# Shifting the start addresses of rounded weights and activations in five feed-forward networks

## The chip, the cores and the metric

One core of one Trainium2 chip. The metric is the device time of the program in microseconds (us). Several runs were timed and their median is quoted; one more execution was recorded by the hardware profiler, and all rows below come from it.

## What is computed

Three transformer layers run one after another on 256 tokens of width 1024. The first mixes with RWKV7 and NSA attention, the second with gated linear attention and FoX, the third with a latent sparse attention. Between them stand five SwiGLU networks: one behind the first layer's mixer, and one on either side of the second's and of the third's. Only these networks and the products around the mixers matter here:

```python
def swiglu(x, w_gate, w_up, w_down):
    return (jax.nn.silu(x @ w_gate) * (x @ w_up)) @ w_down

def swiglu_2(h, w_in, w_out):
    a, b = jnp.split(h @ w_in, 2, axis=-1)
    return (jax.nn.silu(a) * b) @ w_out

for layer in range(DEPTH_2):
    g = norm_g[layer]
    x = x + 0.5 * swiglu_2(rmsnorm(x, g[0]), ffn_w_in[layer, 0], ffn_w_out[layer, 0])
    ...
    x = x + 0.5 * swiglu_2(rmsnorm(x, g[2]), ffn_w_in[layer, 1], ffn_w_out[layer, 1])
```

Everything is float32, with an inner width of 2816.

## The kernel before

Each float32 operand of a large product is split into a rounded high part and a rest, both kept in the rounded 4-byte format `fp32r`, and a product is made of three passes (`PASSES`): high weights with high activations, rest of the weights with high activations, high weights with the rest of the activations. So every 128-by-128 tile of weights costs three matmuls.

A network (`ffn(f, norm)`, f from 0 to 4) is cut into `FC` = 22 chunks of 128 inner columns. For a chunk, the weights arrive by DMA in one slot of `ring` (3,072 floats per partition: 2,048 for gate and up, 1,024 for down). ScalarE rounds them into `w_gu[:, j, 0]` and `w_dn[:, j, 0]` (`hi_a` and `hi_b`, L1368 and L1374), VectorE writes the rests into `w_gu[:, j, 1]` and `w_dn[:, j, 1]` (`lo_a` and `lo_b`, L2028 and L2034); j is the chunk's parity. TensorE then runs `gate_up`: 2 results (gate, up) x 8 blocks k of the inner dimension x 3 passes = 48 matmuls, with a tile of `w_gu` standing in the array and 256 columns of `uT_r` moving through it. `uT_r[0]` is the high part `uT_h` of the normed and transposed activations, `uT_r[1]` the rest `uT_l`. VectorE and ScalarE turn the two results into `h` and its rest (`h_r`), and TensorE runs `down`: 4 parts x 3 passes = 12 matmuls with a tile of `h_r` standing and 512 columns of `w_dn` moving. A chunk is therefore 48 x 256 + 12 x 512 = 18,432 moving columns. In the loop TensorE runs `gate_up` of chunk c, then `down` of chunk c - 1. All matmuls go through one helper, so they carry its line, L498, in the profile; they are told apart by the names of their operands, the moving one first ("uT_h,w_gu": moving `uT_h`, standing `w_gu`).

The mixers' projections use the same three passes. Input projections take the high weights from `in_h`, `even_h` or `odd_h`, and the rest of the weights from `ring_r` (the ring itself, written back in place). Output projections keep a tile of `uT_h` or `uT_l` standing and move 512 columns of `out_h` or `ring_r`. Some small products take `gate_w` (24 columns standing), `odd_small` (8 columns) and, for one sum of FoX, a single column of `fox_head` repeated 128 times.

Addresses. `sb(name, shape)` allocates tensors one after another in each partition, every one at the next multiple of 32 bytes, and `over(name, shape, under, skip)` lays a second, rounded tensor over one of them, `skip` floats past its start. With the sizes of this kernel the tensors start at these bytes (in brackets: bytes past a multiple of 128): `uT` 32,896 (0), `yT` 41,088 (0), `inh` 49,280 (0), `gate_r` 61,568 (0), `ring` 63,104 (0), `ffb` 112,256 (0), `cst` 116,352 (0, with 4,662 floats), `wk` 138,336 (96). `uT_h` lies on `uT`, `uT_l` on `yT`, `in_h` on `inh`, `h_r` on `ffb`; `w_gu`, `w_dn`, `even_h`, `odd_h`, `out_h`, `fox_sum` and `fox_head` lie on `wk` at offsets that are multiples of 128 bytes. The strides from one tile to the next inside these tensors are multiples of 128 bytes, except in `gate_w` (96 bytes) and `odd_small` (32 bytes). So in every network before the change all rounded weights start 96 bytes past a multiple of 128 and all activations on one.

Of the kernel before, what the change touches and what calls it, by code (L numbers as in the profile page):

```python
# [7 lines left out]
F32 = mybir.dt.float32  # L8
F32R = mybir.dt.float32r
U8 = mybir.dt.uint8  # L10
ALU = mybir.AluOpType
# [84 lines left out]
def build(nc, x_in, wstream, gains, consts_in, masks_in, scratch, tri, inv, out):  # L96
    ctx = ExitStack()
    with ctx:
        at = {}

        def sb(name, shape, dt=F32):
            at[name] = nc.sbuf_base
            return ctx.enter_context(nc.sbuf_tensor(name, shape, dt))
# [17 lines left out]

        x = sb("x", [P, TT, D])
        xn = sb("xn", [P, TT, D])
        uT = sb("uT", [P, KC, T])
        yT = sb("yT", [P, KC, T])
        inh = sb("inh", [P, KC * 3 * P])
        gb = inh[:, 0:2 * D].rearrange("p (a b) -> p a b", b=D)
        sb("gate_r", [P, 2 * KC * 24])
        ring = sb("ring", [P, RING, SLOT])
        ffb = sb("ffb", [P, 4, T])  # L130
        cst = sb("cst", [P, NCONST])
        msk = sb("msk", [P, MASKS], U8)
        small = sb("small", [P, 256])
# [16 lines left out]

        ident = C("ident")

        w_gu = over("w_gu", [P, 2, 2, 2 * D], "wk")
        w_dn = over("w_dn", [P, 2, 2, D], "wk", 8 * D)
        h_r = over("h_r", [P, 2, 2, T], "ffb")
        ring_r = over("ring_r", [P, RING, SLOT], "ring")

        w_h = {"even": [over(f"even_h{i}", [P, KC, 3 * P], "wk", o) for i, o in enumerate((17408, 9728))],
# [329 lines left out]
        def slot(i):  # L488
            return ring[:, i % RING, :]
# [3 lines left out]
        def _(pe):  # L493
# [54 lines left out]

            PASSES = [(0, 0), (1, 0), (0, 1)]

            def gate_up(j, between=None):
                for m in range(2):
                    if m and between:
                        between()
                    for k in range(KC):
                        for n, (a, b) in enumerate(PASSES):
                            w = w_gu[:, j % 2, a, (m * KC + k) * P:(m * KC + k + 1) * P]
                            last = mm(ps[4 + 2 * m + j % 2][:, 0:T], w, uT_r[b][:, k, :],
                                      k == 0 and n == 0, k == KC - 1 and n == 2)
                    last.then_inc(s[("gu_gate", "gu_ps")[m]], 1)  # L560

            def first_gate_up(norm):

                for k in range(KC):
                    pe.wait_ge(s["uT_hi"], 16 * TN[norm] + 8 + k + 1)
                    for m in range(2):
                        for a in range(2):
                            mm(ps[4 + 2 * m][:, 0:T], w_gu[:, 0, a, (m * KC + k) * P:(m * KC + k + 1) * P],
                               uT_r[0][:, k, :], k == 0 and a == 0, False)
                for m in range(2):  # L570
                    for k in range(KC):
                        if not m:
                            pe.wait_ge(s["uT_lo"], 16 * TN[norm] + 8 + k + 1)
                        last = mm(ps[4 + 2 * m][:, 0:T], w_gu[:, 0, 0, (m * KC + k) * P:(m * KC + k + 1) * P],
                                  uT_r[1][:, k, :], False, k == KC - 1)
                    last.then_inc(s[("gu_gate", "gu_ps")[m]], 1)

            def spread_rstd(norm):
# [5 lines left out]
                if norm == 1:  # L584
                    mm(ps[1][0:16, 0:384], C("t5")[0:32, :], C("t5_onehot")[0:32, :]).then_inc(s["t5_ps"], 1)

            def down_part(j, t, half, start, stop):
                for n, (a, b) in enumerate(PASSES):
                    last = mm(ps[2 * t + half][:, :], h_r[:, j % 2, a, t * P:(t + 1) * P],
                              w_dn[:, j % 2, b, half * 512:(half + 1) * 512], start and n == 0, stop and n == 2)  # L590
                return last

            def down(j, start):
                for t, half in PARTS:
                    last = down_part(j, t, half, start, False)
                last.then_inc(s["down_done"], 1)

            def ffn(f, norm):
                q = FC * f

                def step(c, r=0):

                    pe.wait_ge(s["lo_a"], r + (q + c + 1))
                    if q + c >= 2:
                        pe.wait_ge(s["h_ready"], r + (q + c - 1))
                    if c == 0:
                        first_gate_up(norm)
                    else:
                        gate_up(c, (lambda: spread_rstd(norm)) if c == 1 else None)
                    if 0 < c < FC - 1:  # L610
                        pe.wait_ge(s["lo_b"], r + (q + c))
                        pe.wait_ge(s["h_ready"], r + (q + c))
                        if norm == 1 and c == 1:
                            pe.wait_ge(s["t5_sb"], 1)
                        down(c - 1, c == 1)
                step(0)
                step(1)
                with pe.Fori(0, 4 * LOOPS, 4) as r:
                    for j in range(4):
                        step(2 + j, r)  # L620
                for c in range(2 + 4 * LOOPS, FC):
                    step(c)

                n = NORM_AFTER_FFN[f]
                pe.wait_ge(s["lo_b"], q + FC - 1)
                pe.wait_ge(s["h_ready"], q + FC - 1)
                for t, half in PARTS[0:3]:
                    down_part(FC - 2, t, half, False, False)
                pe.wait_ge(s["lo_b"], q + FC)
                pe.wait_ge(s["h_ready"], q + FC)  # L630
                for t, half in PARTS[0:3]:
                    down_part(FC - 1, t, half, False, True).then_inc(s["acc_done"], 1)
                first_T(n, 0)
                down_part(FC - 2, 1, 1, False, False).then_inc(s["down_done"], 1)
                down_part(FC - 1, 1, 1, False, True).then_inc(s["down_done"], 1)
                first_T(n, 1)

            def piece(o, j):
# [647 lines left out]
        def _(act):  # L1286
# [676 lines left out]
        def _(v):  # L1963
# [60 lines left out]
            def lo_a(f, c, r=0):  # L2024

                q, i = FC * f, BASE[f"ffn{f}"] + c
                v.wait_ge(s["hi_a"], r + (q + c + 1))
                v.tensor_tensor(w_gu[:, c % 2, 1, :], slot(i)[:, 0:2 * D], w_gu[:, c % 2, 0, :].bitcast(F32),  # L2028
                                ALU.subtract).then_inc(s["lo_a"], 1)

            def lo_b(f, c, r=0):
                q, i = FC * f, BASE[f"ffn{f}"] + c
                v.wait_ge(s["hi_b"], r + (q + c + 1))
                v.tensor_tensor(w_dn[:, c % 2, 1, :], slot(i)[:, 2 * D:3 * D], w_dn[:, c % 2, 0, :].bitcast(F32),  # L2034
                                ALU.subtract).then_inc(s["lo_b"], 1)
                v.wait_ge(s["lo_b"], r + (q + c + 1))
                v.sem_inc(s[f"free{i % RING}"], 1)
# [14 lines left out]
            def ffn(f, scale):  # L2052
                q = FC * f

                def step(c, r=0):
                    n = q + c
                    h, hr = sg[:, c % 2, :], h_r[:, c % 2, :, :]
# [742 lines left out]
```

## Time and profile before

| | |
|---|---|
| median of 3 runs | 1424.02 us (1423.72 to 1424.87) |
| span of the profiled execution | 1422.4 us |
| TensorE matmuls busy | 1395.2 us, 98% |
| TensorE weight loads busy | 1286.2 us, 90% |
| VectorE busy | 944.7 us, 66% |
| ScalarE busy | 691.0 us, 49% |
| mean DMA rate | 168 GB/s |

The span runs from the first to the last instruction of the trace and is 1.6 us under the median of the timed runs. Matmuls overlap one another in the pipeline: one lasts 279 ns with 256 columns, but the next one starts before it ends. So their cost is read from the distance between two starts, not from their duration.

### The profile page before, as it was taken

What the parts mean: (1) busy time and instruction counts of PE and PEld (TensorE: products, weight loads), DVE (VectorE), ACT (ScalarE), POOL (GpSimd) and SP (SyncE); (2) the same over time, 40 slices, a digit from 0 to 9 for tenths busy, and PEclk for the clock granted to TensorE, in tenths of its full rate; (3) what the DMA queues carried; (4) which work ended last, traced back from release to release, by engine and by line L of the source; (5) the groups of instructions that cost most, each with busy time, mean ns of one, the idle gap of its engine ahead of it and who ended that gap; (6) DMA issues with size and microseconds to landing.
All of it is one profiled execution on the core that took longest, in us unless ns stands there. A gap on an engine that the chain in (4) does not pass through costs nothing. (4 is left out here: it accounts for less than half of the span.)

```text
span 1422.4 us, 25483 instructions
## 1 busy us (share of the span) xinstructions
PE 1395.2 (98%) x10044; PEld 1286.2 (90%) x10044; DVE 944.7 (66%) x1539; ACT 691.0 (49%) x1107; POOL 82.9 (6%) x137
## 2 busy tenths in 40 slices
PE   8999999999999999999999999999999999999997
PEld 8898888999989999899989999999998988899997
DVE  5778567766668666567577666676665676676665
ACT  6764545433454443376654433444433655643342
POOL 1030010000020000000000000100000123000000
PEclk9999999999999999999999999999999999999999
DMA  9344005645526555433356545365554423465540
GB/s 359 135 160 185 2 25 228 222 177 183 197 108 228 209 184 177 178 104 133 120 207 224 189 177 182 129 229 198 194 177 178 149 90 134 177 222 180 194 158 30
DMA packets 33069, 239.47 MB, mean 168 GB/s; under 512 B 6864, under 2 KB 13280, under 8 KB 14304
## 3 DMA queue, kind: packets, MB, share of 16 engines
q1 hardware_dynamic: 30320, 234.84, 45.6%
q10 hardware_dynamic: 2672, 3.58, 0.7%
q8 instruction: 51, 0.84, 0.2%
q14 instruction: 26, 0.21, 0.0%
HBM read 236.15 MB, written 2.25 MB: 168 GB/s over the span
## 5 line engine op out<-in xcount | busy, mean ns | idle before, releaser
L498 PE MATMUL ps<-uT_h,w_gu 128*128 128x256 f32 x3520 | 614.1, 279 | 2.5 <-ACT uT_h L1316 2.5
L498 PEld LDWEIGHTS ps<-uT_h,w_gu 128*128 128x128 f32 x3520 | 538.0, 188 | 13.8 <-issue 5.0
L498 PE MATMUL ps<-uT_l,w_gu 128*128 128x256 f32 x1760 | 478.8, 279 | 0.0
L498 PE MATMUL ps<-w_dn,h_r 128*128 128x512 f32 x1320 | 325.7, 396 | 0.3 <-DVE h_r L2070 0.3
L498 PEld LDWEIGHTS ps<-uT_l,w_gu 128*128 128x128 f32 x1760 | 325.5, 188 | 0.0
L498 PEld LDWEIGHTS ps<-w_dn,h_r 128*128 128x128 f32 x1320 | 239.6, 188 | 51.3 <-issue 1.4
L1368 ACT CAST w_gu<-ring 128x2048 fp32r<-128x2048 f32 x110 | 210.0, 1909 | 156.2 <-PE ps L498 155.6
L2028 DVE TENSOR_TENSOR w_gu<-ring,w_gu 128x2048 fp32r<-128x2048 f32 x110 | 252.1, 2292 | 35.2 <-ACT w_gu L1368 35.2
L2061 DVE TENSOR_TENSOR us<-ps,bc 128x256 f32<-128x256 f32 x110 | 46.5, 423 | 203.2 <-PE ps L498 203.2
L1381 ACT ACTIVATE wk<-wk 128x256 f32<-128x256 f32 x110 | 46.1, 419 | 260.7 <-DVE wk L2059 260.7
L1374 ACT CAST w_dn<-ring 128x1024 fp32r<-128x1024 f32 x110 | 115.7, 1052 | 82.8 <-PE ps L498 82.7
L2034 DVE TENSOR_TENSOR w_dn<-ring,w_dn 128x1024 fp32r<-128x1024 f32 x110 | 134.1, 1219 | 5.3 <-ACT w_dn L1374 5.1
L498 PE MATMUL ps<-uT_h,ring_r 128*128 128x256 f32 x408 | 114.4, 281 | 0.0
L498 PE MATMUL ps<-wk 128*128 128x64 f32 (+6 forms) x504 | 76.9, 303 | 1.9 <-DVE small L2337 0.7
L498 PEld LDWEIGHTS ps<-uT_h,ring_r 128*128 128x128 f32 x408 | 77.5, 190 | 0.6 <-issue 0.2
L2059 DVE TENSOR_TENSOR wk<-ps,bc 128x256 f32<-128x256 f32 x110 | 46.7, 425 | 35.8 <-PE ps L498 22.0
L498 PEld LDWEIGHTS ps<-wk 128*128 128x128 f32 (+3 forms) x504 | 56.1, 186 | 7.4 <-issue 2.0
L498 PE MATMUL ps<-ring_r,uT_h 128*128 128x512 f32 (+2 forms) x176 | 62.0, 353 | 0.0
L2064 DVE TENSOR_TENSOR wk<-wk,us 128x256 f32<-128x256 f32 x110 | 46.7, 425 | 7.7 <-ACT wk L1381 4.3
L498 PE MATMUL ps<-uT_h,in_h 128*128 128x256 f32 x176 | 50.5, 289 | 1.0 <-DVE ring_r L2021 1.0
L2070 DVE TENSOR_TENSOR h_r<-wk,h_r 128x256 fp32r<-128x256 f32 x110 | 46.8, 425 | 3.7
L498 PE MATMUL ps<-uT_l,in_h 128*128 128x256 f32 x176 | 48.7, 283 | 0.0
(398 smaller groups left out, 1696.0 us busy)
## 6 DMA issues: line engine op xcount, KB each, us to landing
ring<-wstream SPq DMA_DIRECT2D x144, 1536.0 KB, 6.6
cst<-consts_in SPq DMA_DIRECT2D x1, 2185.0 KB, 13.7
wk<-t_row ACTq DMA_DIRECT2D x1, 2048.0 KB, 8.0
wk<-masks_in SPq DMA_DIRECT2D x1, 1216.0 KB, 24.1
x<-x_in SPq DMA_DIRECT2D x2, 512.0 KB, 4.7
ring<-wstream SPq DMA_DIRECT2D x1, 1024.0 KB, 8.8
inh<-gains ACTq DMA_DIRECT2D x2, 512.0 KB, 9.6
tri_blocks<-wk SPq DMA_DIRECT2D x3, 256.0 KB, 2.8
```

Of the source, the lines that this page charges most:

```text
L498: return pe.matmul(o, l, r, start=start, stop=stop, skip_group_check=True)
L1368: act.copy(w_gu[:, c % 2, 0, :], slot(i)[:, 0:2 * D]).then_inc(s["hi_a"], 1)
L1374: act.copy(w_dn[:, c % 2, 0, :], slot(i)[:, 2 * D:3 * D]).then_inc(s["hi_b"], 1)
L1381: act.activation(sg[:, c % 2, :], sg[:, c % 2, :], ACT.Silu).then_inc(s["silu_ready"], 1)
L2028: v.tensor_tensor(w_gu[:, c % 2, 1, :], slot(i)[:, 0:2 * D], w_gu[:, c % 2, 0, :].bitcast(F32), ALU.subtract).then_inc(s["lo_a"], 1)
L2034: v.tensor_tensor(w_dn[:, c % 2, 1, :], slot(i)[:, 2 * D:3 * D], w_dn[:, c % 2, 0, :].bitcast(F32), ALU.subtract).then_inc(s["lo_b"], 1)
L2059: v.tensor_tensor(h, ps[4 + c % 2][:, 0:T], bc[:], ALU.mult).then_inc(s["gs_ready"], 1)
L2061: v.tensor_tensor(us[:], ps[6 + c % 2][:, 0:T], bc[:], ALU.mult).then_inc(s["us_ready"], 1)
L2064: v.tensor_tensor(h, h, us[:], ALU.mult).then_inc(s["h_mul"], 1)
L2070: v.tensor_tensor(hr[:, 1, :], h, hr[:, 0, :].bitcast(F32), ALU.subtract).then_inc(s["h_ready"], 1)
```

## The change

Three tensors (`uT`, `yT`, `ffb`) are allocated 16 floats longer. Each network gets its own views of the weights and activations: `W_SHIFT` moves `w_gu` and `w_dn` of network f by 8, 0, 24, 0 and 16 floats (32, 0, 96, 0 and 64 bytes), `U_SHIFT` moves `uT_h`, `uT_l` and `h_r` by 0, 8, 0, 16 and 0 floats (0, 32, 0, 64 and 0 bytes). The scratch `sg` lies 32 floats later. The instructions, their order, their sizes and their semaphores stay the same; only operand addresses differ.

```diff
@@ -121,13 +121,13 @@
 
         x = sb("x", [P, TT, D])
         xn = sb("xn", [P, TT, D])
-        uT = sb("uT", [P, KC, T])
-        yT = sb("yT", [P, KC, T])
+        uT = sb("uT", [P, KC * T + 16])[:, 0:KC * T].rearrange("p (k n) -> p k n", k=KC)
+        yT = sb("yT", [P, KC * T + 16])[:, 0:KC * T].rearrange("p (k n) -> p k n", k=KC)
         inh = sb("inh", [P, KC * 3 * P])
         gb = inh[:, 0:2 * D].rearrange("p (a b) -> p a b", b=D)
         sb("gate_r", [P, 2 * KC * 24])
         ring = sb("ring", [P, RING, SLOT])
-        ffb = sb("ffb", [P, 4, T])
+        ffb = sb("ffb", [P, 4 * T + 16])[:, 0:4 * T].rearrange("p (k n) -> p k n", k=4)
         cst = sb("cst", [P, NCONST])
         msk = sb("msk", [P, MASKS], U8)
@@ -150,9 +150,10 @@
 
         ident = C("ident")
 
-        w_gu = over("w_gu", [P, 2, 2, 2 * D], "wk")
-        w_dn = over("w_dn", [P, 2, 2, D], "wk", 8 * D)
-        h_r = over("h_r", [P, 2, 2, T], "ffb")
+        W_SHIFT, U_SHIFT, FFN_OF = (8, 0, 24, 0, 16), (0, 8, 0, 16, 0), {1: 0, 3: 1, 5: 2, 6: 3, 8: 4}
+        w_gu = [over(f"w_gu{f}", [P, 2, 2, 2 * D], "wk", n) for f, n in enumerate(W_SHIFT)]
+        w_dn = [over(f"w_dn{f}", [P, 2, 2, D], "wk", 8 * D + n) for f, n in enumerate(W_SHIFT)]
+        h_r = [over(f"h_r{f}", [P, 2, 2, T], "ffb", n) for f, n in enumerate(U_SHIFT)]
         ring_r = over("ring_r", [P, RING, SLOT], "ring")
 
@@ -163,7 +164,9 @@
         w_small = [over(f"even_small{i}", [P, KC * 40], "wk", 14336 + KC * 40 * i) for i in range(2)]
         wo_h = [over(f"out_h{i}", [P, SLOT], "wk", o) for i, o in enumerate((13312, 17408, 10240))]
         uT_r = [over("uT_h", [P, KC, T], "uT"), over("uT_l", [P, KC, T], "yT")]
-        sg = wk[:, 12 * D:12 * D + 2 * T].rearrange("p (a b) -> p a b", a=2)
+        uT_f = [[over(f"uT_h{f}", [P, KC, T], "uT", n), over(f"uT_l{f}", [P, KC, T], "yT", n)] if n else uT_r
+                for f, n in enumerate(U_SHIFT)]
+        sg = wk[:, 12 * D + 32:12 * D + 32 + 2 * T].rearrange("p (a b) -> p a b", a=2)
         ss = [small[:, 0:1], small[:, 1:2], small[:, 8:9]]
         ss3 = [small[:, 242:243], small[:, 243:244]]
@@ -548,31 +551,32 @@
 
             PASSES = [(0, 0), (1, 0), (0, 1)]
 
-            def gate_up(j, between=None):
+            def gate_up(f, j, between=None):
                 for m in range(2):
                     if m and between:
                         between()
                     for k in range(KC):
                         for n, (a, b) in enumerate(PASSES):
-                            w = w_gu[:, j % 2, a, (m * KC + k) * P:(m * KC + k + 1) * P]
-                            last = mm(ps[4 + 2 * m + j % 2][:, 0:T], w, uT_r[b][:, k, :],
+                            w = w_gu[f][:, j % 2, a, (m * KC + k) * P:(m * KC + k + 1) * P]
+                            last = mm(ps[4 + 2 * m + j % 2][:, 0:T], w, uT_f[f][b][:, k, :],
                                       k == 0 and n == 0, k == KC - 1 and n == 2)
...
@@ -584,15 +588,15 @@
                 if norm == 1:
                     mm(ps[1][0:16, 0:384], C("t5")[0:32, :], C("t5_onehot")[0:32, :]).then_inc(s["t5_ps"], 1)
 
-            def down_part(j, t, half, start, stop):
+            def down_part(f, j, t, half, start, stop):
                 for n, (a, b) in enumerate(PASSES):
-                    last = mm(ps[2 * t + half][:, :], h_r[:, j % 2, a, t * P:(t + 1) * P],
...
@@ -1313,7 +1317,7 @@
                 for c in range(KC):
                     if c % 4 == 0 or t and c % 2 == 0:
                         act.wait_ge(s["xT_ps"], 6 * TN[n] + (2 + c // 2 if t else c // 4) + 1)
-                    act.mul(uT_r[0][:, c, t * P:(t + 1) * P], xT_at(n, t, c), gain_c(n, c)).then_inc(s["uT_hi"], 1)
+                    act.mul(uT_f[FFN_OF.get(n, 0)][0][:, c, t * P:(t + 1) * P], xT_at(n, t, c), gain_c(n, c)).then_inc(s["uT_hi"], 1)
 
             def norm(n):
@@ -1365,13 +1369,13 @@
                 act.wait_ge(s[f"land{i % RING}"], rr + 16 * (i // RING + 1))
                 if q + c >= 2:
                     act.wait_ge(s["gu_ps"], r + (q + c - 1))
-                act.copy(w_gu[:, c % 2, 0, :], slot(i)[:, 0:2 * D]).then_inc(s["hi_a"], 1)
+                act.copy(w_gu[f][:, c % 2, 0, :], slot(i)[:, 0:2 * D]).then_inc(s["hi_a"], 1)
 
             def hi_b(f, c, r=0):
                 q, i = FC * f, BASE[f"ffn{f}"] + c
                 if q + c >= 2:
                     act.wait_ge(s["down_done"], r + (q + c - 1))
-                act.copy(w_dn[:, c % 2, 0, :], slot(i)[:, 2 * D:3 * D]).then_inc(s["hi_b"], 1)
+                act.copy(w_dn[f][:, c % 2, 0, :], slot(i)[:, 2 * D:3 * D]).then_inc(s["hi_b"], 1)
 
             def ffn(f, norm):
...
@@ -1982,8 +1986,9 @@
                         step = 2 if t else 4
                         v.wait_ge(s["uT_hi"], 16 * TN[n] + KC * t + c // step * step + step)
                         tk = slice(t * P, (t + 1) * P)
-                        v.scalar_tensor_tensor(uT_r[1][:, c, tk], xT_at(n, t, c), gain_c(n, c),
-                                               uT_r[0][:, c, tk].bitcast(F32), ALU.mult, ALU.subtract
+                        u = uT_f[FFN_OF.get(n, 0)]
+                        v.scalar_tensor_tensor(u[1][:, c, tk], xT_at(n, t, c), gain_c(n, c),
+                                               u[0][:, c, tk].bitcast(F32), ALU.mult, ALU.subtract
                                                ).then_inc(s["uT_lo"], 1)
 
...
```

The parts left out pass `f` to `gate_up`, `first_gate_up`, `down_part` and `down` and use `w_gu[f]`, `w_dn[f]`, `h_r[f]` and `uT_f[f]` in the same way.

## Rows read from the trace of the kernel before

**Rows 1.** The page, busy time by engine (share of the span, instructions) and clock by slice.

```profile
span 1422.4 us, 25483 instructions
...
PE 1395.2 (98%) x10044; PEld 1286.2 (90%) x10044; DVE 944.7 (66%) x1539; ACT 691.0 (49%) x1107; POOL 82.9 (6%) x137
...
PEclk9999999999999999999999999999999999999999
```

**Rows 2.** Waits of TensorE: engine, line, who released it, us in total, times, longest.

```profile
PE ps L498 <- DMA cst<-consts_in: 5.1, 1, 5.1
PE ps L498 <- DVE xn L1976: 3.3, 3, 1.2
PE ps L498 <- ACT uT_h L1316: 2.5, 5, 0.5
```

**Rows 3.** The five networks' stretches: busy us (instructions) by engine, clock, DMA share, GB/s.

```profile
core 0: us, PE busy (x) PEld busy (x) DVE busy (x) ACT busy (x) POOL busy (x), PEclk, DMA share, GB/s
226.00:413.50 187.50, 187.50 (x1337) 174.57 (x1338) 123.10 (x172) 81.10 (x86) 4.23 (x7) 1.00 0.56 203
...
1229.20:1415.00 185.80, 185.80 (x1324) 173.17 (x1324) 120.79 (x170) 76.81 (x81) 1.49 (x4) 1.00 0.45 165
```

**Rows 4.** Timeline of TensorE, one chunk of network 0: start, length, operation, operands, count.

```profile
258.35 0.40 PE L498 MATMUL ps<-uT_h,w_gu 128*128 128x256 f32 x2
...
263.95 2.96 PE L498 MATMUL ps<-w_dn,h_r 128*128 128x512 f32 x12
266.75 0.40 PE L498 MATMUL ps<-uT_h,w_gu 128*128 128x256 f32 x2
```

**Rows 5.** Timeline of TensorE in the first input projection.

```profile
24.94 0.28 PE L498 MATMUL ps<-uT_h,in_h 128*128 128x256 f32 x1
25.06 0.28 PE L498 MATMUL ps<-uT_h,ring_r 128*128 128x256 f32 x1
25.18 0.28 PE L498 MATMUL ps<-uT_l,in_h 128*128 128x256 f32 x1
...
26.02 0.28 PE L498 MATMUL ps<-uT_h,in_h 128*128 128x256 f32 x1
```

**Rows 6.** Timeline of TensorE in the second and third input projections, far rows.

```profile
613.15 0.28 PE L498 MATMUL ps<-uT_h,even_h 128*128 128x256 f32 x1
...
618.81 0.28 PE L498 MATMUL ps<-uT_h,even_h 128*128 128x256 f32 x1
...
1120.93 0.28 PE L498 MATMUL ps<-uT_h,odd_h 128*128 128x256 f32 x1
...
1126.19 0.28 PE L498 MATMUL ps<-uT_h,odd_h 128*128 128x256 f32 x1
```

**Rows 7.** Timeline of TensorE, products with 24 and 8 standing columns.

```profile
91.98 0.39 PE L498 MATMUL ps<-uT_h,gate_w 128*24 128x256 f32 x2
...
93.00 0.39 PE L498 MATMUL ps<-uT_h,gate_w 128*24 128x256 f32 x2
...
1110.28 0.39 PE L498 MATMUL ps<-uT_h,odd_small 128*8 128x256 f32 x2
...
1110.98 0.39 PE L498 MATMUL ps<-uT_h,odd_small 128*8 128x256 f32 x2
```

**Rows 8.** Timeline of TensorE, the sum with one repeated column standing.

```profile
636.92 1.90 PE L498 MATMUL ps<-fox_sum,fox_head 128*128 128x256 f32 x15
```

**Rows 9.** Groups by line: rounding on ScalarE and VectorE, us busy, mean ns, idle before.

```profile
L1368 ACT CAST w_gu<-ring 128x2048 fp32r<-128x2048 f32 x110 | 210.0, 1909 | 156.2 <-PE ps L498 155.6
L2028 DVE TENSOR_TENSOR w_gu<-ring,w_gu 128x2048 fp32r<-128x2048 f32 x110 | 252.1, 2292 | 35.2 <-ACT w_gu L1368 35.2
```

**Rows 10.** One tile's matmuls: count, ns min/median/max, first and last start.

```profile
L498 PE MATMUL ps<-uT_h,in_h x176: 277/283/468, 15.1 to 91.3; 128*128 128x256 f32 x176
```

More of the change, by code:

```diff
@@ L562, in first_gate_up @@
             def first_gate_up(norm):
+                f = FFN_OF[norm]
                 for k in range(KC):
@@ L567, in first_gate_up @@
                         for a in range(2):
-                            mm(ps[4 + 2 * m][:, 0:T], w_gu[:, 0, a, (m * KC + k) * P:(m * KC + k + 1) * P],
-                               uT_r[0][:, k, :], k == 0 and a == 0, False)
+                            mm(ps[4 + 2 * m][:, 0:T], w_gu[f][:, 0, a, (m * KC + k) * P:(m * KC + k + 1) * P],
+                               uT_f[f][0][:, k, :], k == 0 and a == 0, False)
                 for m in range(2):
@@ L573, in first_gate_up @@
                             pe.wait_ge(s["uT_lo"], 16 * TN[norm] + 8 + k + 1)
-                        last = mm(ps[4 + 2 * m][:, 0:T], w_gu[:, 0, 0, (m * KC + k) * P:(m * KC + k + 1) * P],
-                                  uT_r[1][:, k, :], False, k == KC - 1)
+                        last = mm(ps[4 + 2 * m][:, 0:T], w_gu[f][:, 0, 0, (m * KC + k) * P:(m * KC + k + 1) * P],
+                                  uT_f[f][1][:, k, :], False, k == KC - 1)
                     last.then_inc(s[("gu_gate", "gu_ps")[m]], 1)
@@ L585, in spread_rstd, with down @@
                     mm(ps[1][0:16, 0:384], C("t5")[0:32, :], C("t5_onehot")[0:32, :]).then_inc(s["t5_ps"], 1)
-            def down_part(j, t, half, start, stop):
+            def down_part(f, j, t, half, start, stop):
                 for n, (a, b) in enumerate(PASSES):
-                    last = mm(ps[2 * t + half][:, :], h_r[:, j % 2, a, t * P:(t + 1) * P],
-                              w_dn[:, j % 2, b, half * 512:(half + 1) * 512], start and n == 0, stop and n == 2)
+                    last = mm(ps[2 * t + half][:, :], h_r[f][:, j % 2, a, t * P:(t + 1) * P],
+                              w_dn[f][:, j % 2, b, half * 512:(half + 1) * 512], start and n == 0, stop and n == 2)
                 return last
-            def down(j, start):
+            def down(f, j, start):
                 for t, half in PARTS:
-                    last = down_part(j, t, half, start, False)
+                    last = down_part(f, j, t, half, start, False)
                 last.then_inc(s["down_done"], 1)
@@ L608, in step @@
                     else:
-                        gate_up(c, (lambda: spread_rstd(norm)) if c == 1 else None)
+                        gate_up(f, c, (lambda: spread_rstd(norm)) if c == 1 else None)
                     if 0 < c < FC - 1:
@@ L614, in step @@
                             pe.wait_ge(s["t5_sb"], 1)
-                        down(c - 1, c == 1)
+                        down(f, c - 1, c == 1)
                 step(0)
@@ L627, in ffn @@
                 for t, half in PARTS[0:3]:
-                    down_part(FC - 2, t, half, False, False)
+                    down_part(f, FC - 2, t, half, False, False)
                 pe.wait_ge(s["lo_b"], q + FC)
@@ L631, in ffn @@
                 for t, half in PARTS[0:3]:
-                    down_part(FC - 1, t, half, False, True).then_inc(s["acc_done"], 1)
+                    down_part(f, FC - 1, t, half, False, True).then_inc(s["acc_done"], 1)
                 first_T(n, 0)
-                down_part(FC - 2, 1, 1, False, False).then_inc(s["down_done"], 1)
-                down_part(FC - 1, 1, 1, False, True).then_inc(s["down_done"], 1)
+                down_part(f, FC - 2, 1, 1, False, False).then_inc(s["down_done"], 1)
+                down_part(f, FC - 1, 1, 1, False, True).then_inc(s["down_done"], 1)
                 first_T(n, 1)
@@ L2027, in lo_a @@
                 v.wait_ge(s["hi_a"], r + (q + c + 1))
-                v.tensor_tensor(w_gu[:, c % 2, 1, :], slot(i)[:, 0:2 * D], w_gu[:, c % 2, 0, :].bitcast(F32),
+                v.tensor_tensor(w_gu[f][:, c % 2, 1, :], slot(i)[:, 0:2 * D], w_gu[f][:, c % 2, 0, :].bitcast(F32),
                                 ALU.subtract).then_inc(s["lo_a"], 1)
@@ L2033, in lo_b @@
                 v.wait_ge(s["hi_b"], r + (q + c + 1))
-                v.tensor_tensor(w_dn[:, c % 2, 1, :], slot(i)[:, 2 * D:3 * D], w_dn[:, c % 2, 0, :].bitcast(F32),
+                v.tensor_tensor(w_dn[f][:, c % 2, 1, :], slot(i)[:, 2 * D:3 * D], w_dn[f][:, c % 2, 0, :].bitcast(F32),
                                 ALU.subtract).then_inc(s["lo_b"], 1)
@@ L2056, in step @@
                     n = q + c
-                    h, hr = sg[:, c % 2, :], h_r[:, c % 2, :, :]
+                    h, hr = sg[:, c % 2, :], h_r[f][:, c % 2, :, :]
                     v.wait_ge(s["gu_gate"], r + (n + 1))
```

## The prediction

> **What bounds the kernel.** I read the shares of busy time first, then TensorE's waits, then the stretches of the five networks, and last the distances between matmul starts. TensorE is busy for 1395.2 of 1422.4 us and its clock stands at the full level, 2.4 GHz, in all 40 slices [rows 1]. What it waits for is small and outside the networks' loops: the longest wait is 5.1 us for the constants, the next groups add up to 3.3 and 2.5 us [rows 2]. The first network takes 187.5 us with TensorE busy for 187.50, the last 185.8 with 185.80, and the three between them, whose rows are not shown, lie at 186.4 to 188.5 [rows 3]. VectorE needs 123 us of such a stretch and ScalarE 81 [rows 3]. So inside the networks nothing but the pace of the matmul stream sets the time, and every nanosecond on a matmul arrives at the end.
>
> That pace is what the change can touch. One chunk runs from 258.35 to 266.75 us, 8.40 us [rows 4]. It holds 48 matmuls of 256 columns and 12 of 512, that is 72 units of 256 columns, so 116.7 ns per unit. Its gate and up part alone, 258.35 to 263.95, is 5.60 / 48 = 116.7, and its down part, 263.95 to 266.75, is 2.80 / 24 = 116.7: the same price in both parts. 256 columns at 2.4 GHz are 106.7 ns. So about 10 ns per unit, 9%, is lost somewhere in the stream although nobody waits. A network has 22 x 72 = 1,584 units and all five have 7,920, so 1 ns per unit is 1.6 us in one network and 7.9 us in all.
>
> **Does the loss depend on addresses?** The kernel before has other combinations of the start addresses, and they are not equally fast:
> - The first input projection has weights (`in_h`, `ring_r`) and activations all on multiples of 128 bytes. From 24.94 to 26.02 us there are 9 matmuls, 120.0 ns each, and every distance shown is 0.12 us [rows 5].
> - The networks have weights 96 bytes past and activations on a multiple: 116.7 ns [rows 4].
> - The second and third input projections take two of three weight tiles at 96 bytes past (`even_h`, `odd_h`) and one on a multiple (`ring_r`). 48 matmuls from 613.15 to 618.81 us give 117.9 ns, 45 from 1120.93 to 1126.19 give 116.9 [rows 6].
> - Strides off the multiple: with 24 standing columns 9 matmuls from 91.98 to 93.00 us take 113.3 ns each, with 8 columns 6 from 1110.28 to 1110.98 take 116.7 [rows 7].
> - One repeated column standing, both operands 96 bytes past: 15 matmuls in 1.90 us, of which the last is 0.28 long, so 1.62 / 14 = 115.7 ns [rows 8].
>
> The same shape costs between 113.3 and 120.0 ns at one clock. The order among the full 128-column cases, all equal 120.0, one in three equal 117.9 or 116.9, none equal 116.7, is what one would see if the standing and the moving operand got in each other's way when their addresses agree. I take that as the mechanism. It isn't shown, since these stages also differ in strides.
>
> **Where the change puts things.** The three longer tensors hold 64 bytes more each. So `yT` starts 64 bytes later, everything from `inh` to `ffb` 128 bytes later, and `cst` and what follows, `wk` included, 192 bytes later. `wk` moves from 96 to 32 bytes past a multiple of 128, and the shifts come on top. By network, as weights; `uT_h`, `uT_l`; `h_r`: network 0 has 64; 0, 64; 0. Network 1 has 32; 32, 96; 32. Network 2 has 0; 0, 64; 0. Network 3 has 32; 64, 0; 64. Network 4 has 96; 0, 64; 0. These are not the addresses that the change is described with (0, 96, 64, 96, 32): that list leaves the 192 bytes out.
>
> **The sum.** Two ways to count what "agree" means:
> - Modulo 64. Then networks 0 and 2 have everything on multiples of 64, as the first input projection has, and go from 116.7 to 120.0 ns: 1,584 x 3.3 = 5.2 us each, 10.4 us. Networks 3 and 4 keep weights at an odd and activations at an even multiple of 32, as now: 0. Network 1 has all at odd multiples of 32, which no full-width row shows; its bounds are 113.3 and 120.0 ns, so -5.4 to +5.2 us, and the nearest row, both operands at 96 [rows 8], gives 115.7, or -1.6 us. That row has hardly any weights to read, so I take 0. The first input projection stays on multiples of 64: 0.
> - Modulo 128. Networks 1 and 2 have weights and `uT_h` alike in two passes of three and weights and `h_r` alike in all. With 3.3 ns for all three passes, 2.2 for two and 1.1 for one, the gate and up part costs 1,056 x 2.2 = 2.3 us and the down part 528 x 3.3 = 1.7 us, 4.1 us (from unrounded terms) per network and 8.1 for two. In network 0 only `uT_l` is like the weights: 1,056 x 1.1 = 1.2 us. Networks 3 and 4 have no like pair: 0. In the first input projection `uT_l` leaves the multiple: it has 176 matmuls of each pass with `in_h` [rows 10], and with 16 output-side ones per pass some 576 in all, at -1.1 ns, -0.6 us. Together +8.7 us.
>
> Both come to about the same, and I take 9.5 us. The profiled span would go from 1422.4 to 1431.9 us and the median, 1.6 us above it, from 1424.0 to 1433.5 us. Network 1 alone moves this by 5 us, and if only network 2 pays it is 4: 1428 to 1439 for this case.
>
> **Edits costed at nothing.** No instruction, wait or transfer is added. ScalarE's rounding of a chunk's gate and up weights takes 1,909 ns and VectorE's rest 2,292 ns [rows 9], in a chunk of 8.40 us; ScalarE and VectorE have 106 and 64 us of slack per network [rows 3]. If a shifted output made each of these a tenth slower, 0.2 us per chunk, that slack would cover it. The cover is gone only if the matmuls got faster by a third. The output projections and the second and third input projections read `wk` at 32 instead of 96 bytes past: for both ways of counting that is no new agreement with the activations on a multiple, 0; a change of 1 ns on their some 1,500 units would be 1.5 us. The later place of `sg`, a whole 128 bytes, changes nothing in any of this.
>
> The Trainium skill speaks against the whole mechanism. Its page SBUF — State Buffer says under Specifications (TRN2) that SBUF is read in 16-byte lines, and under Who interferes with whom that TensorE has separate read ports for the moving and the standing operand and never waits on anyone. All shifts are multiples of 32 bytes, so by it a start would stay on a line and the result would be no change, 1424.0 us. This trace does not settle it, but 120.0 against 116.7 ns [rows 4, 5] is a difference that this rule leaves unexplained. The page TensorE: Matmul & The Clock Gate gives under Back-to-back issue gap N/2.4 + 2.5 ns, 109.2 ns for 256 columns; an estimate by it would put the most that five networks could gain at 7,920 x 7.5 ns, about 59 us. No row reaches that.
>
> **The rivals.**
> - Nothing depends on these addresses, and the 120.0 ns come from something else in that stage, such as its 1,536-byte stride between tiles. For it: the five networks lie within 1.5% of each other, and the down part, whose operands have other roles and strides, pays the same 116.7. Against it: the second input projection has the same 1,536-byte stride and 117.9. Time: 1424.0 us.
> - Faster. Some distance between the streams that the kernel never had at full width (64 bytes, or 32 on the other side) is cheaper than today's. The place is the three networks with such a distance, 0, 3 and 4, and with network 1 four of five are new in some pair. The price goes down to the 113.3 ns of [rows 7]: 1,584 x 3.4 = 5.4 us per network. Two such networks and no dear one give 1424.0 - 10.8 = 1413.2 us; all five give 1397. It decides as soon as the networks that win outnumber those that lose. For it: 113.3 was reached with mixed residues. Against it: only with 24 columns to load, and 8 columns gave 116.7.
> - The change isn't what it is called, since the pads move `wk`. If the addresses were those of its name, networks 0 and 2 would still be the ones with all on multiples of 64, and modulo 64 the sum is the same 10.4 us. So this rival has no time of its own.
>
> **How the numbers follow.** Agreement costs, slower: 0.50, at 1433.5 us. No dependence, or gains and losses that cancel: 0.20, at 1424.0. Faster: 0.30, at 1413. What a measurement of this kernel can tell from no change is about 0.2%, 2.8 us. The range of 8 in 10 runs from 1411 us, where the two-network gain is held and only larger ones are out, to 1440 us, where network 1 pays in full.
>
> **What would show it.** In the profile after, the length of one chunk in each network: 8.40 us today, 8.64 us (72 x 120.0 ns) in networks 0 and 2 if modulo 64 is right, about 8.6 in 1 and 2 if modulo 128 is right, 8.40 in 3 and 4. If all five stay at 8.40 us, addresses don't matter. If any shows less than 8.35, there is a cheaper distance and the forecast's sign is in doubt. The clock has to stay at its full level, and waits of TensorE in the networks have to stay near zero; otherwise the cause is another.

## The result

The changed kernel takes 1428.12 us (median), the kernel before 1424.85 us in the same session; the ratio is 1.0023 with a 95% interval of 1.0014 to 1.0033. It is slower by 3.3 us. The forecast was slower by 9.5 us: the side is right, the size is almost three times too large, and, as the experiments show, most of the reasons behind it are wrong. All times compared below are of undisturbed executions; one of the ten of the first scan took 4854 us, where the others took 1427 to 1429, and is left out of its interval.

The page of the profile after, busy time and clock, is close to [rows 1], with 4.5 us more of TensorE:

```profile
span 1426.7 us, 25483 instructions
...
PE 1399.7 (98%) x10044; PEld 1293.5 (91%) x10044; DVE 945.4 (66%) x1539; ACT 689.6 (48%) x1107; POOL 82.7 (6%) x137
...
PEclk9999999999999999999999999999999999999999
```

The waits of TensorE (engine and line, who released it, us in total, times, longest) are those of [rows 2] to 0.1 us, so no large wait was added:

```profile
PE ps L501 <- DMA cst<-consts_in: 5.1, 1, 5.1
PE ps L501 <- DVE xn L1980: 3.2, 3, 1.2
PE ps L501 <- ACT uT_h L1320: 2.5, 5, 0.5
```

The time is in the pace of the matmuls. This is the timeline of TensorE in the changed kernel, one chunk of each network, read as [rows 4]: the first line of three is the start of gate and up, the second the start of down, the third the start of the next chunk.

```profile
318.21 0.40 PE L501 MATMUL ps<-uT_h,w_gu 128*128 128x256 f32 x2
...
323.86 2.93 PE L501 MATMUL ps<-w_dn,h_r 128*128 128x512 f32 x12
326.63 0.40 PE L501 MATMUL ps<-uT_h,w_gu 128*128 128x256 f32 x2
...
507.98 0.40 PE L501 MATMUL ps<-uT_h,w_gu 128*128 128x256 f32 x2
...
513.63 2.88 PE L501 MATMUL ps<-w_dn,h_r 128*128 128x512 f32 x12
516.35 0.40 PE L501 MATMUL ps<-uT_h,w_gu 128*128 128x256 f32 x2
...
818.36 0.40 PE L501 MATMUL ps<-uT_h,w_gu 128*128 128x256 f32 x2
...
824.00 2.94 PE L501 MATMUL ps<-w_dn,h_r 128*128 128x512 f32 x12
826.78 0.40 PE L501 MATMUL ps<-uT_h,w_gu 128*128 128x256 f32 x2
...
1007.75 0.40 PE L501 MATMUL ps<-uT_h,w_gu 128*128 128x256 f32 x2
...
1013.45 2.96 PE L501 MATMUL ps<-w_dn,h_r 128*128 128x512 f32 x12
1016.25 0.40 PE L501 MATMUL ps<-uT_h,w_gu 128*128 128x256 f32 x2
...
1323.47 0.40 PE L501 MATMUL ps<-uT_h,w_gu 128*128 128x256 f32 x2
...
1329.13 2.96 PE L501 MATMUL ps<-w_dn,h_r 128*128 128x512 f32 x12
1331.93 0.40 PE L501 MATMUL ps<-uT_h,w_gu 128*128 128x256 f32 x2
```

The chunks last 8.42, 8.37, 8.42, 8.50 and 8.46 us; every one was 8.40 before, as in [rows 4]; the rows of the other four aren't shown. Network 1 is faster, the others are slower. The table has the median over some 20 chunks of each network, per 256 columns, worked out from the starts in the trace like this: gate and up is first start to second start over 48, down is second to third over 24. In network 3 two kinds of chunk alternate (118.7 and 118.4 ns in gate and up, 116.5 and 116.2 in down), and the row has their middle. Distances are weights minus the other operand, modulo 256 bytes; why 256 comes with the experiments.

| network | weights - `uT_h`, `uT_l` | gate and up, ns | weights - `h_r` | down, ns | chunk, us | against before |
|---|---|---|---|---|---|---|
| before, all five | 224, 224 | 116.7 | 224 | 116.7 | 8.400 | |
| 0 | 192, 128 | 117.7 | 64 | 115.4 | 8.420 | +0.020 |
| 1 | 128, 64 | 117.8 | 0 | 113.3 | 8.373 | -0.027 |
| 2 | 0, 192 | 117.7 | 128 | 115.8 | 8.427 | +0.027 |
| 3 | 96, 32 | 118.5 | 224 | 116.4 | 8.484 | +0.084 |
| 4 | 224, 160 | 118.0 | 96 | 116.5 | 8.460 | +0.060 |

The last column sums to 0.164 us, times 22 chunks 3.6 us, near the 3.3 us of the medians. Gate and up lost in every network, between 1.0 and 1.9 ns, and down won in all five, from 0.1 to 3.4 ns. The first input projection [rows 5], at 120.0 ns before in its earlier and later parts alike, now has two paces. From 24.87 to 33.59 us 72 matmuls take 121.1 ns each, and from 66.95 to 68.01 us 9 take 117.8:

```profile
24.87 0.28 PE L501 MATMUL ps<-uT_h,in_h 128*128 128x256 f32 x1
...
33.59 0.28 PE L501 MATMUL ps<-uT_h,in_h 128*128 128x256 f32 x1
...
66.95 0.28 PE L501 MATMUL ps<-uT_h,in_h 128*128 128x256 f32 x1
...
68.01 0.28 PE L501 MATMUL ps<-uT_h,in_h 128*128 128x256 f32 x1
```

Over the whole stage the two nearly cancel: about -0.3 us, an estimate from the lengths of the stretches.

### The profile page after: what moved, and what is told of

Read it like the earlier page. It is cut to its first block and busy times, and to the rows that moved or that the text cites. A ratio compares the mean times of both kernels' runs of the same rounds, so it can differ in the third digit from the quotient of the medians.

```text
span 1426.7 us, 25483 instructions
## 1 busy us (share of the span) xinstructions
PE 1399.7 (98%) x10044; PEld 1293.5 (91%) x10044; DVE 945.4 (66%) x1539; ACT 689.6 (48%) x1107; POOL 82.7 (6%) x137
## 5 line engine op out<-in xcount | busy, mean ns | idle before, releaser
L1378 ACT CAST w_dn<-ring 128x1024 fp32r<-128x1024 f32 x110 | 115.4, 1049 | 81.4 <-PE ps L501 81.3
L501 PE MATMUL ps<-uT_h,ring_r 128*128 128x256 f32 x408 | 114.2, 281 | 0.0
```

The costliest lines, as they stand in the source:

```text
L501: return pe.matmul(o, l, r, start=start, stop=stop, skip_group_check=True)
L1378: act.copy(w_dn[f][:, c % 2, 0, :], slot(i)[:, 2 * D:3 * D]).then_inc(s["hi_b"], 1)
```

## The experiments

### Undoing one part: `uT_l` back beside `uT_h`

```diff
-        uT = sb("uT", [P, KC * T + 16])...
-        yT = sb("yT", [P, KC * T + 16])...
+        uT = sb("uT", [P, KC * T + 32])...
+        yT = sb("yT", [P, KC * T + 32])...
```

> The changed kernel with one thing undone: `uT` and `yT` are 32 floats longer instead of 16, so `uT_l` is back on a multiple of 128 bytes like `uT_h`; `wk`, all weights, `uT_h` and `h_r` keep the residues of the changed kernel. Theory 1 (the 64 bytes between `uT_h` and `uT_l`, a side effect of the pads, make the gate and up part dearer): gate and up fall to about 116.8 ns per 256 columns in all five networks, the down part stays as in the changed kernel, so chunks of about 8.37, 8.33, 8.38, 8.39, 8.40 us and a total of about 3 us below the kernel before. Theory 2 (my forecast: weights and activations that agree cost 120 ns): networks 1 and 2, where all agree, show 120 ns in gate and up and chunks of 8.5 us; the total stays above the kernel before.

Measured: 1429.18 us against 1424.79, ratio 1.0038 (1.0024 to 1.0053). Neither theory holds. Chunks are 8.400, 8.373, 8.520, 8.48 and 8.50 us. Network 2 (timeline of TensorE):

```profile
817.28 0.40 PE L508 MATMUL ps<-uT_h,w_gu 128*128 128x256 f32 x2
...
823.03 2.94 PE L508 MATMUL ps<-w_dn,h_r 128*128 128x512 f32 x12
825.80 0.40 PE L508 MATMUL ps<-uT_h,w_gu 128*128 128x256 f32 x2
```

5.75 / 48 = 119.8 ns in gate and up, as my forecast's theory wanted where all agree modulo 128. But network 1 agrees just as well and shows 117.8 ns in gate and up, and 113.3 in down. Network 4 has weights 96 past a multiple of 128 and the rest on one, as in the kernel before, and shows 118.5 and 117.2 ns (the middle of two kinds of chunk that alternate, as in network 3 above) instead of 116.7 and 116.7. So 128 is not the modulus. The longer tensors had also moved `wk` and `ffb` by 128 bytes against `uT`, which the expectation had taken for nothing.

### One part alone: the pads without the shifts

The kernel before with `uT`, `yT` and `ffb` 16 floats longer, no view moved.

> The kernel before with only the three 16-float pads, no shift at all. Every network then has weights 32 bytes past a multiple of 128, `uT_h` 0, `uT_l` 64, `h_r` 0. Theory 1: gate and up at about 118 ns in all five, chunks of 8.46 us, total about 6 us over the kernel before. Theory 2 (agreement of weights and activations): nothing agrees, chunks of 8.40 us, total within 1 us of the kernel before.

Measured: 1431.35 us against 1424.79, ratio 1.0047 (1.0030 to 1.0064), and five equal networks:

```profile
508.98 0.40 PE L498 MATMUL ps<-uT_h,w_gu 128*128 128x256 f32 x2
...
514.65 2.96 PE L498 MATMUL ps<-w_dn,h_r 128*128 128x512 f32 x12
517.45 0.40 PE L498 MATMUL ps<-uT_h,w_gu 128*128 128x256 f32 x2
```

5.67 / 48 = 118.1 ns and a chunk of 8.47 us, where my forecast's theory had 8.40. Theory 1 has all its numbers right here, and yet the run before and the next one speak against it: with both activation parts alike, gate and up didn't fall to 116.8. So the pads alone, which the change needs only to make room, cost 6.6 us; the shifts on top of them gave 3.3 us back. Nothing agrees with anything here modulo 128, and still the pace is worse than before.

### A grid of other combinations

`W_SHIFT` = (24, 8, 16, 16, 0), activations (0, 8, 0, 24, 0), `h_r` (8, 0, 8, 16, 8) floats, with the pads of the first experiment.

> Five other combinations, as weights; activations (both parts alike); `h_r`, in bytes past a multiple of 128: network 0 has 0; 0; 32, network 1 has 64; 32; 0, network 2 has 96; 0; 32, network 3 has 96; 96; 64, network 4 has 32; 0; 32. Theory 1: gate and up near 116.8 ns in all five, since both activation parts agree with each other. Theory 2: 120 ns in networks 0 and 3, 116.8 elsewhere. For the down part both expect 227 ns per 512 columns in network 4, as network 1 of the changed kernel has with 32 and 32; what 0 and 32, 64 and 0, 96 and 32, 96 and 64 give is open between 227 and 240.

Measured, as network: distance to `uT_h`, to `uT_l`: gate and up; distance to `h_r`: down. 0: 128, 0: 120.0; 96: 116.1. 1: 32, 160: 117.2; 64: 115.0. 2: 96, 224: 118.4; 64: 114.8. 3: 0, 128: 117.8; 32: 116.6. 4: 32, 160: 117.1; 0: 114.2. (1427.88 us against 1424.79, a single run, so without an interval.) Theory 1 is out by 0.3 to 3.2 ns. Theory 2 holds in network 0, and is out by 2.2 ns in network 3 and by 0.3 to 1.6 in the others. Set beside the runs so far, all distances taken modulo 256, the rows come near each other. The down part shows 113.3, 113.3 and 114.2 at distance 0, 115.4, 114.7, 115.0 and 114.8 at 64, 115.8 and 115.6 at 128, 116.7, 116.4 and 116.4 at 224; it is loosest at 96, with 116.5, 117.2 and 116.1. Gate and up at (0, 128) shows 117.8 and 117.8, at (128, 0) 119.7 and 120.0, at (32, 160) 117.2 and 117.1. That became the new theory: the distance between the two operands modulo 256 sets the pace. For the down part agreement is the cheapest distance, the opposite of what I had assumed. Rows of one distance still differ by up to 1.1 ns, so the theory was rough from the start.

### Scanning the distance

For these the activations stay where the kernel before has them, no tensor is longer, and only the weights move (`sg` makes room for them).

```diff
-        W_SHIFT, U_SHIFT, FFN_OF = (8, 0, 24, 0, 16), (0, 8, 0, 16, 0), ...
+        W_SHIFT, U_SHIFT, H_SHIFT, FFN_OF = (16, 8, 32, 24, 40), (0, 0, 0, 0, 0), (0, 0, 0, 0, 0), ...
```

> The kernel before without any pad, with only the weights of each network moved (activations, `h_r`, projections and everything else stay where they were). `uT_h`, `uT_l` and `h_r` all start 128 bytes past a multiple of 256; the weights of networks 0 to 4 start 32, 0, 96, 64 and 128 bytes after them, modulo 256. Theory A (the distance from activations to weights modulo 256 decides, and one law holds for both parts): the down part shows per 256 columns about 116.5, 113.3, 116.5, 115, 115.7 ns as in the runs so far, and gate and up follow the same order with network 1 the cheapest, near 113.3 ns. Theory B (my forecast: agreement is dear in gate and up, as the first input projection's 120.0 ns suggests, whatever the down part does): gate and up of network 1 at 120.0 ns, 5.76 us per chunk. Theory C (only the residue modulo 128 counts): network 4 equals network 1 in both parts.

The second run has `W_SHIFT` = (56, 48, 8, 0, 72).

> The same with other distances: weights 192, 160, 0, 224 and 0 + 256 bytes after the activations. Network 3 has exactly the addresses of the kernel before and should show its 8.40 us chunk whatever the theory. Networks 2 and 4 differ by a whole 256 bytes: if the modulus is 256 they show the same, and the same as network 1 of the other run; if it is 512 or more they differ. 192 and 160 are new at these equal activations; theory A expects for them the order that the down part shows, which has not been seen there either.

| distance of weights, bytes modulo 256 | 0 | 32 | 64 | 96 | 128 | 160 | 192 | 224 (before) |
|---|---|---|---|---|---|---|---|---|
| gate and up, ns per 256 columns | 119.8 | 118.4 | 113.9 | 117.4 | 118.7 | 119.9 | 117.8 | 116.7 |
| down, ns per 256 columns | 114.5 | 116.5 | 114.5 | 117.3 | 115.7 | 116.7 | 116.7 | 116.7 |

Networks 1 and 3 of the first run (timeline of TensorE), distances 0 and 64:

```profile
509.25 0.40 PE L501 MATMUL ps<-uT_h,w_gu 128*128 128x256 f32 x2
...
515.01 2.91 PE L501 MATMUL ps<-w_dn,h_r 128*128 128x512 f32 x12
517.75 0.40 PE L501 MATMUL ps<-uT_h,w_gu 128*128 128x256 f32 x2
...
1008.41 0.40 PE L501 MATMUL ps<-uT_h,w_gu 128*128 128x256 f32 x2
...
1013.87 2.91 PE L501 MATMUL ps<-w_dn,h_r 128*128 128x512 f32 x12
1016.62 0.40 PE L501 MATMUL ps<-uT_h,w_gu 128*128 128x256 f32 x2
```

5.76 / 48 = 120.0 ns against 5.46 / 48 = 113.8: at one clock and with one instruction stream, 64 bytes of address make 0.29 us per chunk. Network 1 of the second run, distance 160, is as dear in gate and up, 5.75 / 48 = 119.8, but not cheap in down:

```profile
510.06 0.40 PE L501 MATMUL ps<-uT_h,w_gu 128*128 128x256 f32 x2
...
515.81 2.96 PE L501 MATMUL ps<-w_dn,h_r 128*128 128x512 f32 x12
518.61 0.40 PE L501 MATMUL ps<-uT_h,w_gu 128*128 128x256 f32 x2
```

The distance 0 was measured in three networks, one of them 256 bytes further on, and gave 119.8 and 114.5 ns each time; network 3 of the second run, with the addresses of before, gave 116.7 and 116.7. The modulus is 256 as far as this tells. Theory C, 128, is dead (0 and 128 differ in both parts), theory B is right on its one point, 120 ns at distance 0 in gate and up, and theory A is wrong in one: the two parts don't follow one law, 0 is dear in gate and up and cheap in down. The totals, 1428.04 and 1433.37 us against 1424.82 (ratios 1.0024, 1.0014 to 1.0034, and 1.0060, 1.0043 to 1.0077), are 3.2 and 8.6 us above it; the chunks make 2.5 and 8.9.

### Distance or place

```diff
+        sb("ahead", [P, 16])
         uT = sb("uT", [P, KC, T])
```

> The kernel before with 16 unused floats allocated ahead of `uT`, so that `uT`, `yT`, `inh`, `ring`, `ffb`, `wk` and all that lies on them start 64 bytes later, together. Distances between operands stay, residues all change. Theory A (only the distance modulo 256 from the moving or standing activations to the weights counts): every network keeps its 8.40 us chunk, 116.7 ns in both parts, and the first input projection its 120.0 ns; total as before. Rival (the residue of each operand by itself counts, for example against a fixed slot of the memory): chunks change, as they did when 64 bytes were added to one operand only, by up to 0.15 us, and the total by up to 15 us.

Measured: 1424.50 us against 1424.62, ratio 1.000 (0.999 to 1.0009). Network 1:

```profile
507.73 0.40 PE L499 MATMUL ps<-uT_h,w_gu 128*128 128x256 f32 x2
...
513.33 2.96 PE L499 MATMUL ps<-w_dn,h_r 128*128 128x512 f32 x12
516.13 0.40 PE L499 MATMUL ps<-uT_h,w_gu 128*128 128x256 f32 x2
```

All five networks show 116.7 and 116.7 ns. 64 bytes on every operand change nothing; the pads, which moved `uT_l`, `h_r` and the weights by 64, 128 and 192 bytes against `uT_h`, changed 6.6 us. As far as one shift of 64 bytes can tell, the place doesn't count, the distance does.

### All networks at 64

`W_SHIFT` = (24, 24, 24, 24, 24), the rest as in the scans.

> The kernel before with the weights of all five networks 96 bytes later, nothing else: 64 bytes after the activations modulo 256, as network 3 of scan_1. Theory A: every chunk 8.21 us (48 x 113.9 + 24 x 114.5 ns) instead of 8.40, 110 x 0.187 = 20.5 us, total about 1404 us. Rival (network 3 of scan_1 was fast for another reason, such as its neighbours' addresses or its place in the program): the others don't follow it and the total falls by less than 8 us.

Measured: 1406.09 us against 1424.62, ratio 0.9876 (0.9861 to 0.9891), 18.5 us faster, where theory A had 20.5 from the chunks. All five networks have chunks of 8.21 us; here network 1:

```profile
500.80 0.40 PE L501 MATMUL ps<-uT_h,w_gu 128*128 128x256 f32 x2
...
506.27 2.91 PE L501 MATMUL ps<-w_dn,h_r 128*128 128x512 f32 x12
509.01 0.40 PE L501 MATMUL ps<-uT_h,w_gu 128*128 128x256 f32 x2
```

### The same by layout, and a miss

```diff
-        yT = sb("yT", [P, KC, T])
+        yT = sb("yT", [P, KC * T + 16])...
-        ffb = sb("ffb", [P, 4, T])
+        ffb = sb("ffb", [P, 4 * T + 8])...
```

> The kernel before with `yT` 16 floats and `ffb` 8 floats longer and no shifted view: `in_h` and `ring_r` move 64 bytes against the activations, `wk` 96, `h_r` 64. Every full-width product of the rounded format then has weights 64 bytes after the activations, modulo 256, except the down part, where weights and `h_r` agree. Theory A: chunks of 8.21 us in the networks (113.9 and 114.5 ns), 113.9 instead of 120.0 ns in the first input projection (576 matmuls, 3.5 us), about 114 instead of 117 to 118 in the other two (some 900 matmuls, 3 us), 228 to 229 instead of 233.5 ns in the output projections (288 matmuls, 1.4 us): about 28 us less than before, 1396 to 1397 us. Rival: the projections, which mix tensors and strides of 1,536 bytes, don't follow the networks' law and the total stays near the 1404 us of w_64.

Measured: 1418.78 us against 1424.62, ratio 0.9959 (0.9945 to 0.9972). Theory A had 1396 to 1397 us and the rival 1404; both were missed. The first blocks of the input projection did fall to 113.4 ns (later ones ran at 113.5 to 113.8 or at 117.7 to 118.0), but gate and up in the networks ran at 117.8 ns although its distance is 64, with down at 113.3: chunks of 8.373 us. Network 1:

```profile
505.02 0.40 PE L498 MATMUL ps<-uT_h,w_gu 128*128 128x256 f32 x2
...
510.67 2.88 PE L498 MATMUL ps<-w_dn,h_r 128*128 128x512 f32 x12
513.39 0.40 PE L498 MATMUL ps<-uT_h,w_gu 128*128 128x256 f32 x2
```

The law of the distance, part by part, had failed. The one thing in which these networks differ from those of w_64, besides moved neighbours, is `h_r`, now at distance 0.

> w_64 with one more operand moved: `h_r` 64 bytes later, so that weights and `h_r` agree modulo 256 while weights stay 64 bytes after both activation parts. This is what separates the networks of layout_64 (gate and up 117.8 ns) from those of w_64 (113.9 ns). Theory L (gate and up at this distance can run at two paces, and the stream that comes before, the down part, decides which): gate and up 117.8 ns, down 113.3 ns, chunks of 8.37 us, total about 1421 us. Theory A as it stood (each part's distance alone decides): gate and up 113.9, down 113.3 to 114.5 ns, chunks of 8.19 us, total about 1403 us; then layout_64 was slow for another reason, such as the moved ring.

The edit against w_64:

```diff
-        ffb = sb("ffb", [P, 4 * T + 0])...
+        ffb = sb("ffb", [P, 4 * T + 16])...
-        W_SHIFT = (24, 24, 24, 24, 24), H_SHIFT = (0, 0, 0, 0, 0)
+        W_SHIFT = (8, 8, 8, 8, 8), H_SHIFT = (16, 16, 16, 16, 16)
```

(The pad moves `wk` by 64 bytes, so the weights are where w_64 has them against the activations.) Measured: 1421.45 us against 1424.59, ratio 0.9977 (0.9968 to 0.9987). Network 1:

```profile
506.86 0.40 PE L501 MATMUL ps<-uT_h,w_gu 128*128 128x256 f32 x2
...
512.51 2.88 PE L501 MATMUL ps<-w_dn,h_r 128*128 128x512 f32 x12
515.23 0.40 PE L501 MATMUL ps<-uT_h,w_gu 128*128 128x256 f32 x2
```

5.65 / 48 = 117.7 ns in gate and up, 2.72 / 24 = 113.3 in down, in all five networks. Moving the operand that gate and up doesn't read made gate and up slower by 3.9 ns per 256 columns and down faster by 1.2. So one distance allows more than one pace in gate and up, and the placing of the other part's operand takes part in which one it is. That this works through the down part's stream running ahead of gate and up, as theory L has it, fits but isn't shown apart.

### All products at 64

```diff
         yT = sb("yT", [P, KC, T])
+        ffb = sb("ffb", [P, 4, T])
+        sb("ahead", [P, 16])
         ...
         ring = sb("ring", [P, RING, SLOT])
-        ffb = sb("ffb", [P, 4, T])
+        sb("ahead2", [P, 8])
         cst = sb("cst", [P, NCONST])
```

> layout_64 with `h_r` 64 bytes before the weights as well: `ffb` is allocated right behind `yT`, 16 unused floats follow and 8 more stand ahead of `cst`. No shifted views. All full-width products of the rounded format, the output and input projections included, have weights 64 bytes after activations or `h_r`. Theory L: networks as in w_64 (chunks of 8.21 us, 18.5 us less in all, as w_64 measured), the projections at 113.4 ns wherever they settle at the fast pace as about half of them did in layout_64, worth 2 to 6 us more: 1400 to 1404 us. Theory A with a slow ring: networks at 8.37 us, total as layout_64, 1419 us.

Measured: 1404.28 us against 1424.59, ratio 0.9859 (0.9842 to 0.9875), 20.3 us faster, with chunks of 8.21 us in all networks. Its median is the lowest of the study, though its interval overlaps that of w_64. The pace of the networks also settles a point that the scans left open: moving the weights alone moves them against `ring` too, from which they are rounded. Weights minus `ring` is 64 bytes in w_64 and 0 here, and the paces are the same, so that distance isn't what sets them. The first input projection shows two paces side by side (timeline of TensorE, the same tensors and distances in both stretches):

```profile
25.27 0.28 PE L500 MATMUL ps<-uT_h,in_h 128*128 128x256 f32 x1
...
27.75 0.28 PE L500 MATMUL ps<-uT_h,in_h 128*128 128x256 f32 x1
...
66.88 0.28 PE L500 MATMUL ps<-uT_h,in_h 128*128 128x256 f32 x1
...
68.24 0.28 PE L500 MATMUL ps<-uT_h,in_h 128*128 128x256 f32 x1
```

21 matmuls from 25.27 to 27.75 us are 118.1 ns each, 12 from 66.88 to 68.24 are 113.3. (The rounding of a start to 10 ns is worth 0.5 and 0.8 ns here; unrounded they are 117.8 and 113.3.) In this projection each such stretch begins behind a wait or behind a few other, smaller products, and keeps its pace until the next break. The 2 to 6 us that I had hoped for from the projections came to 1.8 by the medians, which the intervals don't tell from nothing.

## Why the prediction was right and wrong

**What bounds the kernel** was read rightly. TensorE hardly waits in the networks' loops, 1 ns per 256 columns is 7.9 us in all five, and the sum of the chunks gives the total of every run within 3 us.

**Addresses matter**: right, and the rival of no dependence (0.20) is out. It is the one thing that [rows 4, 5] had rightly pointed to, and the runs show it where only addresses differ. What the Trainium skill states on its page SBUF — State Buffer, that TensorE never waits on anyone (Who interferes with whom) and that SBUF is read in 16-byte lines (Specifications (TRN2)), would have given no change. It can't tell 113.9 from 119.8 ns, with all starts a multiple of 32 bytes apart; here the measurement decides.

**What "agree" means** is the step that failed. Both ways to count, modulo 64 and modulo 128, were taken from stages in which only two distances of full-width tiles occur, 0 and 224, and the trace couldn't tell a modulus from them. With them fell the price in the sum, 3.3 ns for every unit in which operands agree and nothing for the rest. In bytes modulo 256 the first input projection stands at 0 and the networks before at 224, but 32 of the scan is as near to 0 on the other side and costs 118.4, and 160, which agrees with nothing, costs as much as 0. Of the seven distances of the scan that the networks didn't have before, "agreement is dear, all else is as today" had one right in gate and up, distance 0.

**The terms.** Network 2 was to pay 4.1 to 5.2 us, with everything alike modulo 64; it has distances 0, 192 and 128 and paid 0.6 (0.027 x 22). Network 0 was to pay 1.2 to 5.2 and paid 0.4. Network 1 had 0 or 4.1 and won 0.6. Networks 3 and 4 stood at 0 in both counts and paid 1.8 and 1.3, most of the loss. So the total of 3.6 from the chunks came together from other places than the 9.5 forecast, and that the side came out right is luck.

**The down part** was priced with a number from gate and up (3.3 ns for agreement). The sign is the other way: weights and `h_r` at distance 0 run at 113.3 to 114.5 ns, as cheap as any that was seen. In the changed kernel this and its neighbours are what kept the loss small: up to 24 x 3.4 ns = 0.08 us per chunk.

**The 192 bytes** of the pads I did count, and they decide more than the shifts: alone they cost 6.6 us. But I had them as a detail of where things land, not as an edit with a price of its own; modulo 256 they took all distances of the network, not one, to new values. I also wrote that the first input projection would keep its pace by one count and gain 0.6 us by the other; its earlier blocks lost about 1 ns and its later ones won about 2, and neither count has a place for both.

**The faster rival** (0.30) named 113.3 ns at some distance that the kernel never had. Such a distance exists, 64, and it is worth 18.5 us for all networks, not the 27 us of the rival's floor. Its condition was not met: the change brings distance 64 only into network 1, for `uT_l` alone, and network 0's `h_r`.

**The 59 us** that the prediction gives as the most that could be gained take the N/2.4 + 2.5 ns of the Trainium skill, page TensorE: Matmul & The Clock Gate, section Back-to-back issue gap, as the pace of a stream. The page gives it for a single isolated matmul. The best run here won 20.3 us, and its networks still stand at 113.9 and 114.5 ns.

**What stays open.** Why a distance sets a pace isn't shown by any run. Nor is it shown why chunks of two kinds alternate in some networks (118.7 and 118.4 ns in network 3 of the changed kernel), although the two halves of every buffer lie a multiple of 256 bytes apart: distances modulo 256 are not the whole account. The runs have one profile each, so whether a stretch takes the same pace in every execution isn't known. Distances under 32 bytes apart weren't tried. Nor is it known which of its paces each distance of the scan has shown: gate and up at 0, 32 or 160 may have a faster one too.

## What to carry to other kernels

When TensorE never waits, measure the distance between matmul starts against columns over clock, stage by stage: where the surplus, here 6 to 12%, differs between stages of one shape, try where the tensors lie. Here that was worth up to 20.3 us of 1424.6, and at least 6% of surplus stayed in every run. Scan the distance between the standing and the moving operand modulo 256 bytes at the kernel's own shapes, each network or stage at another value in one run, and take the whole loop's time, since moving one part's operand changed the other part's pace here. And a pad that only makes room moves every tensor behind it, so it is an edit with a price.

## What the runs showed of the hardware

- The pace of `fp32r` matmuls with a full tile of weights at 2.4 GHz lay between 113.3 and 120.0 ns per 256 columns in the networks once a network had settled, never at the 106.7 of the clock. It depended on the distance between the operands' addresses and not on their place (64 bytes on all of them: 116.7 and 116.7 ns, unchanged); distances 0 and 256 bytes gave the same 119.8 and 114.5 ns.
- The dependence isn't the same for both shapes. At distance 0 the 256-column stream took 119.8 and the 512-column stream 114.5 ns per 256 columns.
- One distance has more than one pace: with the same operands 12 matmuls in a row ran at 113.3 ns in one stretch and 21 at 118 in another, and moving only `h_r` turned gate and up from 113.9 to 117.8 ns.
